# The last expert's sums of a streaming encoder: one-hot products and plain writes in place of two indirect additions

## The reference, cut to what matters

```python
def moe_ffn(x, w_r, wg, wu, wd):
    B, L, D = x.shape
    xt = x.reshape(-1, D)
    logits = jnp.dot(xt, w_r, preferred_element_type=F32)
    top_v, top_i = lax.top_k(logits, TOP_K)
    w = jax.nn.softmax(top_v, axis=-1)
    gates = jnp.einsum('tk,tke->te', w, jax.nn.one_hot(top_i, N_EXPERTS, dtype=F32))
    y = jnp.zeros(xt.shape, F32)
    for e in range(N_EXPERTS):
        h = jax.nn.silu(xt @ wg[e]) * (xt @ wu[e])
        y = y + gates[:, e:e + 1] * jnp.dot(h, wd[e], preferred_element_type=F32)
    return y.astype(x.dtype).reshape(B, L, D)
...
    x = x + jnp.concatenate([y_a, y_b, y_c], axis=-1) @ w_out
    x = x + ffn(rmsnorm(x, g_ffn))
```

## Time and profile before

| what | us |
|---|---|
| median of 3 runs | 1599.54 |
| lowest and highest | 1597.89, 1600.13 |
| profiled execution, device time | 1600.71 |
| its span, from the first to the last instruction | 1598.9 |
| TensorE busy in the span | 1543.5 |
| end of TensorE's last matmul | 1584.8 |

### The profile page before, as it was taken

How to read it: one execution, slowest core, us unless ns; L and a number is a source line. 1 busy time by engine, 2 the same in 40 slices (tenths; PEclk the granted TensorE clock), 3 DMA queues, 4 the chain that set the end, 5 groups by cost and what they waited for, 6 DMA issues and landing times.

```text
span 1598.9 us, 21494 instructions
## 1 busy us (share of the span) xinstructions
PE 1543.5 (97%) x8368; PEld 1340.2 (84%) x8368; DVE 1234.5 (77%) x1245; ACT 999.7 (63%) x1078; POOL 232.1 (15%) x270
## 2 busy tenths in 40 slices
PE   6999899999998998999999999999999999999996
PEld 5988899999998885888888888888888888888885
DVE  4866566663467665898898898898898898898994
ACT  4554433333446444777777777777777777777774
POOL 4802320000051132311001002002002002002000
PEclk9999999999999998999999999999999999999998
DMA  6432544444434248999999999999999999999992
GB/s 178 132 105 80 109 131 146 158 159 155 134 107 144 67 105 281 335 377 369 396 367 364 386 375 369 397 368 373 382 370 378 380 372 369 395 366 365 395 359 87
DMA packets 159027, 435.10 MB, mean 272 GB/s; under 512 B 12295, under 2 KB 66387, under 8 KB 144592
## 3 DMA queue, kind: packets, MB, share of 16 engines
q1 hardware_dynamic: 150708, 420.40, 73.0%
q0 software_dynamic: 5968, 9.93, 2.4%
q10 hardware_dynamic: 2252, 3.41, 0.7%
HBM read 428.09 MB, written 13.34 MB: 276 GB/s over the span
## 4 chain that ended last, share of the span: by engine, by line
PE 86%; DVE 5%; ACT 4%; DMA 2%; issue 1%; POOL 1%; ACTq 0%; POOLq 0%; DVEq 0%
PE bank L1864 26%; PE bank L2319 13%; PE bank L2321 13%; PE bank L2326 13%; PE bank L2335 6%; PE bank L2332 6%; PE bank L2341 6%; DVE cut_lo L1265 2%; ACT cut_hi L868 2%; PE bank L2350 2%; PE bank L1867 2%; DMA ring<-ffn_w_up 1%; DMA ring<-w_in 1%; ACT pe L967 1%; POOL acc L668 1%
## 5 line engine op out<-in xcount | busy, mean ns | idle before, releaser
L1701 DVE TENSOR_TENSOR split_lo<-raw,split_hi 128x2048 fp32r<-128x2048 f32 x336 | 762.9, 2288 | 104.1 <-ACT split_hi L1134 103.1
L1134 ACT CAST split_hi<-raw 128x2048 fp32r<-128x2048 f32 x336 | 640.7, 1911 | 228.5 <-PE bank L2326 149.0
L2319 PE MATMUL bank<-split_hi,xgT_hi 128*128 128x512 f32 x896 | 291.5, 395 | 1.5 <-DVE xgT_lo L1716 1.5
L2321 PE MATMUL bank<-split_hi,xgT_lo 128*128 128x512 f32 x896 | 286.8, 390 | 0.0
L1265 DVE TENSOR_TENSOR cut_lo<-ring,cut_hi 128x1024 fp32r<-128x1024 f32 x124 | 154.2, 1245 | 140.2 <-ACT cut_hi L868 140.2
L1864 PE MATMUL bank<-xT_hi,cut_hi 128*128 128x320 f32 x752 | 242.4, 322 | 6.7 <-DVE cut_lo L1265 3.2
L2326 PE MATMUL bank<-split_lo,xgT_hi 128*128 128x512 f32 x896 | 239.8, 389 | 0.0
L868 ACT CAST cut_hi<-ring 128x1024 fp32r<-128x1024 f32 x124 | 129.6, 1048 | 175.3 <-PE bank L1864 167.7
L1864 PE MATMUL bank<-xT_lo,cut_hi 128*128 128x320 f32 x752 | 235.1, 313 | 0.0
L1864 PE MATMUL bank<-xT_hi,cut_lo 128*128 128x320 f32 x752 | 235.0, 313 | 0.0
L2326 PEld LDWEIGHTS bank<-split_lo,xgT_hi 128*128 128x128 f32 x896 | 168.2, 188 | 35.1
(11 more groups left out here) (285 smaller groups left out, 1692.5 us busy)
## 6 DMA issues: line engine op xcount, KB each, us to landing
raw<-moe_w_gate SPq DMA_DIRECT2D x112, 1024.0 KB, 8.0
raw<-moe_w_up SPq DMA_DIRECT2D x112, 1024.0 KB, 7.7
raw<-moe_w_down SPq DMA_DIRECT2D x112, 1024.0 KB, 7.5
ring<-w_in SPq DMA_DIRECT2D x15, 1024.0 KB, 5.5
ring<-ffn_w_gate SPq DMA_DIRECT2D x11, 1024.0 KB, 5.6
ring<-ffn_w_up SPq DMA_DIRECT2D x11, 1024.0 KB, 5.4
ring<-ffn_w_down SPq DMA_DIRECT2D x10, 1024.0 KB, 5.0
ring<-w_out SPq DMA_DIRECT2D x8, 1024.0 KB, 5.0
```

Source lines behind the costliest of these rows:

```text
L1134: return nc.scalar.copy(split_hi[:, i % SR, :], raw_piece(i)).then_inc(hi_ready, 1)
L1701: V.tensor_tensor(split_lo[:, i % SR, :], raw_piece(i), split_hi[:, i % SR, :].bitcast(F32), ALU.subtract).then_inc(lo_ready, 1)
L2319: TE.matmul(o, xgT_hi[:, kk, :], hi[:, w * k + 512 * c:w * k + 512 * c + 512], start=kk == 0, stop=False)
L2321: TE.matmul(o, xgT_lo[:, kk, :], hi[:, w * k + 512 * c:w * k + 512 * c + 512], start=False, stop=False)
```

## The change

The last expert's sums no longer go through ye and indirect additions. While the last expert still runs, SyncE reads y_p and y_s, with the sums of the seven experts before, back into the tile x. VectorE compares the last expert's token numbers with 1 to 320 and so makes last_hot, a 128 x 320 matrix of zeros and ones in which row p has its one at row p's token. ScalarE scales the sums as before, but into a high part (last_y_hi, in the place of xgT_hi), VectorE makes the low part (last_y_lo), and TensorE multiplies last_hot's 128, 128 and 64 columns by both parts, which spreads the sums over the tokens, in banks 0 to 2 for the first half of the features and 3 to 5 for the second. VectorE adds the six banks to x, and SyncE writes each of the six pieces of x to y_p or y_s as soon as it is summed. GpSimd ends its work with the seventh expert's rows.

```diff
@@ sync
             if more > 0: ...
+
+            sp.wait_ge(rows_out, more * 64 + NE // 2 * 64)
+            sp.dma_start(x[:, 0:2, :], y_p[0].rearrange("(t p) d -> p t d", p=P)).then_inc(y_back, 16)
+            sp.dma_start(x[0:DEC, 2, :], y_s[0]).then_inc(y_back, 16)
+            for half, c in enumerate(HALVES):
+                for t, (t0, rows) in enumerate(TILES):
+                    sp.wait_ge(y_summed, NT * half + t + 1)
+                    sp.dma_start(y_rows_of(t, c), x[0:rows, t, c]).then_inc(y_out, 16)
+            sp.wait_ge(y_out, 16 * 2 * NT)
@@ gpsimd
             with pool.Fori(1, pairs * 2) as n:
                 turn(n, False)
-            add_rows(pairs * 2 - 1)
-            pool.wait_ge(rows_out, pairs * 64 + 32)
+            pool.wait_ge(rows_out, pairs * 64)
@@ scalar
-            y_copy(pairs, -1)
+            nc.scalar.copy(last_token[:], slots[:, bass.ds(pairs * 2 - 1, 1), 0:1].rearrange("p n w -> p (n w)")).then_inc(last_token_ready, 1)
+            act.wait_ge(t_free, pairs * 18 + 2)
+            act.wait_ge(piece_used, pairs * (2 * NP) + SR)
+            for half, c in enumerate(HALVES):
+                nc.scalar.activation(last_y_hi[:, c], banks[6 + half][:], ACT.Copy, scale=now_w[:, 1, 1:2]).then_inc(last_hi, 1)
@@ vector
+            dve.wait_ge(last_token_ready, 1)
+            V.tensor_scalar(last_hot[:, 0:T], C("slot")[:, 1:T + 1], last_token[:, 0:1], None, ALU.is_equal).then_inc(last_hot_ready, 1)
+            for half, c in enumerate(HALVES):
+                dve.wait_ge(last_hi, half + 1)
+                V.scalar_tensor_tensor(out=last_y_lo[:, c], in0=banks[6 + half][:], scalar=now_w[:, 1, 1:2], in1=last_y_hi[:, c].bitcast(F32),
+                                       op0=ALU.mult, op1=ALU.subtract).then_inc(last_lo, 1)
+            dve.wait_ge(y_back, 32)
+            for half, c in enumerate(HALVES):
+                for t, (t0, rows) in enumerate(TILES):
+                    dve.wait_ge(last_full, NT * half + t + 1)
+                    V.tensor_tensor(x[0:rows, t, c], x[0:rows, t, c], banks[NT * half + t][0:rows, :], ALU.add).then_inc(y_summed, 1)
@@ tensor
+            pe.wait_ge(t_free, pairs * 18 + 2)
+            pe.wait_ge(last_hot_ready, 1)
+            for half, c in enumerate(HALVES):
+                pe.wait_ge(last_hi, half + 1)
+                for t, (t0, rows) in enumerate(TILES):
+                    TE.matmul(banks[NT * half + t][0:rows, :], last_hot[:, t0:t0 + rows], last_y_hi[:, c], start=True, stop=False)
+                pe.wait_ge(last_lo, half + 1)
+                for t, (t0, rows) in enumerate(TILES):
+                    TE.matmul(banks[NT * half + t][0:rows, :], last_hot[:, t0:t0 + rows], last_y_lo[:, c], start=False, stop=True).then_inc(last_full, 1)
```

More of the change, by code:

```diff
@@ L447, in build @@
         isc_s = sb("isc_s", [P, 1], U32)
-        sb("below_xg", [P, 48])
+        last_token = sb("last_token", [P, 1])
+        sb("below_xg", [P, 47])
         xg = sb("xg", [P, D])
@@ L452, in build @@
         hs = sb("hs", [P, 2, 512])
-        Gown = sb("Gown", [P, NT, P])
+        first_only = ExitStack()
+        Gown = sb("Gown", [P, NT, P], F32, first_only)
+        first_only.close()
+        last_hot = sb("last_hot", [P, NT * P], FR)
         sb("below_hmT_lo", [P, 384])
@@ L490, in build @@
         g_free, u_free = sem("g_free"), sem("u_free")
+        last_token_ready, last_hot_ready, last_hi, last_lo = sem("last_token_ready"), sem("last_hot_ready"), sem("last_hi"), sem("last_lo")
+        y_back, last_full, y_summed, y_out = sem("y_back"), sem("last_full"), sem("y_summed"), sem("y_out")
         t_full, t_free, y_free = sem("t_full"), sem("t_free"), sem("y_free")
@@ L548, in outputs_left, with y_rows_of @@
             eng.wait_ge(cv_out, 16 * 4 * DEPTH)
+        HALVES = [slice(0, 512), slice(512, 1024)]
+        last_y_hi = xgT_hi[:].rearrange("p k n -> p (k n)")
+        last_y_lo = xgT_lo[:].rearrange("p k n -> p (k n)")
+        def y_rows_of(t, c):
+            return y_p[0, P * t:P * t + P, c] if t < 2 else y_s[0, :, c]
         block = ctx.enter_context(nc.Block())
```

## The result

The changed kernel takes 1613.97 us (median of 4 runs, 1612.03 to 1614.82) against 1598.97 us for the kernel before (4 runs). The ratio is 1.010, with a 95% interval of 1.0085 to 1.0115: 15 us slower. The forecast was 5 us faster, with 1598.4 as the upper end of its range.

The account below looks back on a forecast made before the run. TensorE, busy 97% of the 1598.9 us span, bounds the kernel; behind its last matmul 0.1 + 1.3 + 0.9 + 3.9 + 2.35 + 0.55 = 9.1 us replace 14.1, 5.0 less: median 1594.5 us, range 1592.8 to 1598.4.

Parts of the forecast that it names:

- the time up to the last matmul: TensorE's stretch through its last loop matmul: same instructions in the same order, so no change.
- D: At the end, plain writes go no faster than the added rows did, 100 GB/s: 3.8 us slower, 1603.3; chance 0.04.
- Scaling and low parts: Behind the last matmul: 0.1 us wait, 1.3 us scaling on ScalarE, 0.9 us rest of the low parts on VectorE.
- the additions: Six VectorE additions of the banks to x at the end, 0.65 us apart: 3.9 us, the longest new piece.
- a write of 128 KB: SyncE's last of six writes, 64 rows of 2 KB: lands 2.3 us after issue.
- Rival B: At the end, the six writes land late, after 4.8 us instead of 2.3: gain 2.5 us, 1597.0; chance 0.14.
- The DRAIN: GpSimd's closing DRAIN moves ahead of the end, beside TensorE's work: 4.8 of the 5.0 us gained.
- rival A: The forecast itself: GpSimd's DRAIN goes out of the path at the end, -5.0 us; chance 0.70.
- C: The 4.8 us DRAIN at the end isn't GpSimd's and moves to SyncE: gain 0.3 us, 1599.2; chance 0.11.
- The read-back: SyncE reads 1.31 MB during the last expert, ending near 1572.5, 14 us before the first add: price nothing.
- TensorE's first one-hot product: After the loop, TensorE's exit costs nothing; a gap of more than 1 us would make this wrong.
- The granted clock: During the one-hot products at the end, a fall to half clock would cost 0.3 us.

Follow-up runs that it names:

- e1: The changed kernel with filler below_xg at 40 words instead of 47, so xg to hmT_lo stand at their old addresses: 1592.97 us, ratio 0.9966.
- e2: The kernel before with below_xg at 56 words instead of 48, so xg to hmT_lo stand 32 bytes higher: 1619.21 us, ratio 1.0125.
- e3: As e1, and GpSimd also waits for the six plain writes before it ends: 1596.83 us, ratio 0.9982.
- e6: The kernel before with hmT_lo alone 32 bytes higher: 1602.99 us, ratio 1.0033.
- e9: The kernel before with every tile from hmT_hi to hmT_lo, stationary and moving together, 32 bytes higher: 1598.78 us, ratio 1.0009.
- e4: The kernel before, with SyncE instead of GpSimd waiting for the last expert's two indirect additions: 1595.34 us, ratio 0.9979.

## Why the prediction was wrong

**The step that failed** is in its first paragraph: "the instructions up to its last matmul stay the same and in the same order. So the question is what lies behind that matmul." The instructions are the same, but they read other addresses. So the sum put the time up to the last matmul at no change, without looking at the addresses, and it grew by 18.5 us; this is the term that failed. I compared the order of the instructions and read the two numbers of the filler (48 and 47) as a swap of one word; the tiles' addresses in the built program would have shown the 32 bytes. No rival covered it. Even the slow one, D, looked for its loss at the end, and its mechanism didn't occur: the plain writes moved 270 to 350 GB/s in each us from 1607 to 1611, not 100. The cost is 17.0 us on the gate and up products and 5.8 on the down products. e1 and e2 show it from both sides: their medians stand 26.2 us apart, of which the six lines hold 20.9 (1238.0 against 1217.1 us) and the end 5.2.

**What held**, step by step of the forecast, measured in the changed kernel:

- Behind the last matmul 9.1 us were forecast and 8.9 came. Scaling and low parts end 2.17 us after the last matmul (2.3 forecast), the additions take 3.67 us (3.9), a write of 128 KB lands after 2.5 us (2.3). The rule of the Trainium skill that the prediction cites for this write (DMA: Bandwidth & Descriptors, Anatomy of one DMA) is given there for transfers that GpSimd issues; SyncE's write came near the 2.3 us estimated from it. Rival B, a landing of 4.1 us or more, is out with these 2.5 us. (The upper end that the prediction gives B, 1598.2, would need a landing of 6.0 us, for which it names no row.)
- The DRAIN, the bulk of the gain (rival A against C): 4605 ns on GpSimd beside TensorE's work, 13 ns on SyncE at the end. e3 puts it back: from the landing to the end of its span it needs 5.0 us (1592.1 to 1597.1), e1 0.4 (1589.7 to 1590.1). The 4.6 us between them are what was expected; the medians stand 3.9 us apart. Rival C is out. The Trainium skill's "~12 ns constant" (VectorE: DVE Perf Modes, The DRAIN you can't avoid) fits SyncE's 13 ns here and not GpSimd's 4605. The prediction took it to speak for rival C; but 12 ns on all engines would leave no engine with a cost to move.
- The read-back was issued at 1584.9, 18 us ahead of the end of the last matmul as forecast, and landed after 5.0 and 5.7 us, so some 14 us before the first addition had need of it. It cost nothing. TensorE's first one-hot product began 0.87 us after its last loop matmul, within the 1 us that the prediction allowed.
- The granted clock did not fall under TensorE's small products: 1.00 until 1611. The prediction had allowed 0.3 us for a fall.
- With the addresses put right (e1) the time is 1592.97 us, and the forecast for the mechanism was 1594.5 with 1593 to 1596.6 around it; by ratio, 0.34% gained (0.21 to 0.48) against 0.31% forecast. For the tail the forecast was right by its mechanism and not by luck; for the whole kernel it was wrong.

**What stays open.** Why the distance matters. Weight loads stand beside matmuls in the timelines, so TensorE seems to load the next stationary tile while the present one's moving rows are read; that the two reads meet in SBUF when their distance is off a multiple of 256 bytes would be one reason. No run shows this, only the rule itself, for float32r tiles of these sizes. A plain pair rule (a matmul is slow when the tile loaded beside it is off) doesn't fit e6, where hmT_lo alone is off. The four matmuls of L2341 in a row all load from hmT_hi and read split_lo, both in their old places. Yet the starts in e6's trace lie 231.2 ns apart from the second to the third and 233.7 from the third to the fourth (means of 111 groups), against 226.9 and 226.7 in the kernel before, though none of these loads is from hmT_lo. One tile that is off slows its neighbours too, and what carries this over isn't known. Distances other than 0, 32, 64 and 128 modulo 256 and -32 and -128 weren't tried.

## What to carry to other kernels

Before forecasting from the order of instructions, compare the addresses of all tiles in the two built programs: a one-word tile takes 32 bytes, and where a kernel keeps filler tiles, ask what they hold in place; here it was worth some 20 us, and the new code 5. Where TensorE is the bound and streams weights, keep the distance between stationary and moving tiles at a multiple of 256 bytes; with float32r products of 128x512 it was worth 1.2 to 1.4% of the time here. And let an engine with a costly close-down finish early: in this kernel the last wait is better on SyncE than on GpSimd.

## What the runs showed of the hardware

- Matmuls of 128x512 with float32r operands: 6.3 ns more each (17.0 us over 2688) in the gate and up products and 4.3 ns (5.8 us over 1344) in the down products, of which only hmT_lo was off, with the granted clock at 1.00 and the same 1.5 us of idle time in either case.
- 128 bytes off costs the gate and up products 14.6 us, 32 bytes 17.0, and 256 bytes nothing (817.8 us against 818.1).
- Moved together by 32 bytes, stationary and moving tiles cost nothing (e9, ratio 1.0009); the address itself doesn't matter.
- GpSimd's DRAIN at the end of the block took 4605 ns after a hundred us without work, 4768 ns right after its transfers had landed, and 8932 ns when it began while they were being issued (e4); SyncE's took 13 to 48 ns.
